# Behind the experts: row statistics on ScalarE, the first values block between the transposes, outputs stored by tile

## The reference

```
x <- LN(a*x + mixer(x));  x <- LN(a*x + memory_cross_attention(x));  x <- LN(a*x + grouped_moe(x))

def post_norm(x, h, g, b):
    z = (DN_ALPHA * x + h).astype(F32)
    mu = jnp.mean(z, axis=-1, keepdims=True)
    var = jnp.mean(jnp.square(z - mu), axis=-1, keepdims=True)
    z = (z - mu) * lax.rsqrt(var + LN_EPS)
    return (z * g.astype(F32) + b.astype(F32)).astype(x.dtype)

def gla_mixer(x, s0, w_in, w_gk2, b_gk2, norm_g, w_out):   # token mixer of layer two
    proj = x @ w_in
    q, k, v, gate, lr = jnp.split(proj, [hk, 2 * hk, 2 * hk + hv, 2 * hk + hv + D_MODEL], axis=-1)
    gk = jax.nn.log_sigmoid((lr @ w_gk2 + b_gk2).astype(F32)) / B_GATE_NORMALIZER
    ...
```

## Time and profile before

| | |
|---|---|
| median of 3 runs | 1459.6 us (1458.09 to 1459.87) |
| profiled execution, its own time | 1458.91 us |
| span of that execution, first to last instruction | 1457.2 us |
| mean granted TensorE clock | 0.987 of 2.4 GHz |
| busy: TensorE, VectorE, ScalarE, POOL | 1374.1, 1034.4, 749.1, 121.2 us |
| HBM traffic over the span | 235 GB/s |

### The profile page before, as it was taken

How to read it: one execution, slowest core, us unless ns; L and a number is a source line. 1 busy time by engine, 2 the same in 40 slices (tenths; PEclk the granted TensorE clock), 3 DMA queues, 4 the chain that set the end, 5 groups by cost and what they waited for, 6 DMA issues and landing times.

```text
span 1457.2 us, 19818 instructions
## 1 busy us (share of the span) xinstructions
PE 1374.1 (94%) x7772; PEld 1145.4 (79%) x7772; DVE 1034.4 (71%) x1121; ACT 749.1 (51%) x764; POOL 121.2 (8%) x195
## 2 busy tenths in 40 slices
PE   6999999999889999999998999999889999999993
PEld 5879898779767788888886988679767788888882
DVE  4444776683548889898987555781658989898985
ACT  4344643333433777676773532331424776676761
POOL 6000045400000000000000023100000000000000
PEclk9999999999999999999999999999999999999997
DMA  8774454434873699888882354445872799898961
GB/s 245 258 238 148 146 189 123 142 108 181 341 310 116 257 335 335 327 338 321 340 319 97 103 185 165 150 151 201 322 286 87 297 326 343 328 331 332 334 246 37
DMA packets 99682, 343.71 MB, mean 236 GB/s; under 512 B 5968, under 2 KB 32096, under 8 KB 70416
## 3 DMA queue, kind: packets, MB, share of 16 engines
q1 hardware_dynamic: 96048, 330.59, 63.1%
q0 software_dynamic: 3552, 11.99, 2.6%
HBM read 327.61 MB, written 14.94 MB: 235 GB/s over the span
## 4 chain that ended last, share of the span: by engine, by line
PE 81%; DVE 11%; ACT 4%; issue 1%; DMA 1%; POOL 0%; SPq 0%; DVEq 0%; ACTq 0%
PE ps L1668 63%; PE ps L1981 2%; PE ps L2126 2%; DVE x L1149 1%; DVE x L1146 1%; DVE stats L1125 1%; PE ps L2168 1%; PE ps L1751 1%; PE ps L2003 1%; PE ps L2038 1%; DVE mix_s L1391 1%; PE ps L1677 1%; PE ps L1991 1%; PE ps L2068 1%; PE ps L1676 1%
## 5 line engine op out<-in xcount | busy, mean ns | idle before, releaser
L1668 PE MATMUL ps<-w_hi,xt_hi 128*128 128x512 f32 x704 | 280.6, 399 | 13.5 <-DVE w_lo L1088 7.7
L1668 PE MATMUL ps<-w_hi,xt_lo 128*128 128x512 f32 x704 | 276.7, 393 | 0.0
L1088 DVE TENSOR_TENSOR w_lo<-raw,w_hi 128x2048 fp32r<-128x2048 f32 x68 | 155.4, 2294 | 158.6 <-ACT w_hi L732 158.6
L1668 PE MATMUL ps<-w_lo,xt_hi 128*128 128x512 f32 x640 | 251.6, 393 | 0.0
L732 ACT ACTIVATE w_hi<-raw 128x2048 fp32r<-128x2048 f32 x68 | 129.3, 1913 | 175.2 <-PE ps L1668 88.0
L1092 DVE TENSOR_TENSOR moe_lo<-moe_in_raw,w_hi 128x2048 fp32r<-128x2048 f32 x72 | 164.3, 2290 | 30.2 <-ACT w_hi L739 30.1
L1092 DVE TENSOR_TENSOR w_lo<-raw,w_hi 128x2048 fp32r<-128x2048 f32 x72 | 164.9, 2292 | 27.4 <-ACT w_hi L739 26.9
L1668 PEld LDWEIGHTS ps<-w_hi,xt_hi 128*128 128x128 f32 x704 | 133.3, 189 | 44.6 <-issue 8.5
L739 ACT ACTIVATE w_hi<-moe_in_raw 128x2048 fp32r<-128x2048 f32 x72 | 138.4, 1922 | 50.4 <-PE ps L1668 50.4
L1668 PEld LDWEIGHTS ps<-w_hi,xt_lo 128*128 128x128 f32 x704 | 133.0, 189 | 29.7
L739 ACT ACTIVATE w_hi<-raw 128x2048 fp32r<-128x2048 f32 x72 | 137.4, 1911 | 12.6 <-PE ps L1668 12.6
(11 more groups left out here) (369 smaller groups left out, 2370.8 us busy)
## 6 DMA issues: line engine op xcount, KB each, us to landing
raw<-in_moe_w_gate SPq DMA_DIRECT2D x48, 1024.0 KB, 4.9
moe_in_raw<-in_moe_w_down SPq DMA_DIRECT2D x48, 1024.0 KB, 4.9
moe_in_raw<-in_moe_w_up SPq DMA_DIRECT2D x32, 1024.0 KB, 4.9
raw<-in_moe_w_up SPq DMA_DIRECT2D x32, 1024.0 KB, 4.9
raw<-in_xattn_w_kv SPq DMA_DIRECT2D x16, 1024.0 KB, 5.9
raw<-in_hgrn_w_in SPq DMA_DIRECT2D x16, 1024.0 KB, 5.6
raw<-in_cache_mem_k SPq DMA_DIRECT2D x16, 1024.0 KB, 5.0
moe_in_raw<-in_moe_w_gate SPq DMA_DIRECT2D x16, 1024.0 KB, 4.9
```

What stands on the lines that cost most here:

```text
L1088: nc.vector.tensor_tensor(lo_at(slot_of(k)), raw_at(slot_of(k)), hi_at(hi_slot(k)).bitcast(F32), ALU.subtract).then_inc(w_low, 1)
L1668: ins = mm(out, lhs, rhs, start=start and n == 0, stop=stop and n == 2, skip_group_check=shared)
```

## The change

Four things, all behind the experts.

1. The third norm's row statistics go from VectorE to ScalarE (`tile_sums`): a Copy with scale -1/1024 that also sums (the negated mean), a Square with that as bias that also sums, Ln, Exp. VectorE keeps scale and shift (`tile_scale`). ScalarE starts a tile when that tile's two sums are added.
2. The splits of layer two's first three chunks move into the last visit of layer one's experts (`split_next`).
3. Layer two's blocks run v, v, k, q, gate, gate. The first values block runs by row tile between the transposes (`turn_next`, `first_values`); the transposes go to other banks (`turn_bank0`). Behind it come the low-rank product and the second values block, with the four decay products in its middle, two PSUM banks in place of four; decay work of ScalarE and VectorE goes behind the two values blocks, key and query products from the first values block to the first gate block.
4. The outputs are stored by row tile from SP, each when its tile is done.

The diff, without the lines that only follow from these:

```diff
 def block_kind(l, n):
-    kinds = [("f", 2), ("v", 2), ("q", 2), ("gate", 2)] if l == 0 else [("k", 1), ("q", 1), ("v", 2), ("gate", 2)]
+    kinds = [("f", 2), ("v", 2), ("q", 2), ("gate", 2)] if l == 0 else [("v", 2), ("k", 1), ("q", 1), ("gate", 2)]
...
 def turns(u, t):
+def turn_bank0(u, t):
+    return (4, 6, 3)[t] if u == 4 else (0, 2, 7)[t]
 def at(static, groups, per):
...
+            for t in range(TILES):
+                sp.wait_ge(ln_done, TILES * (3 * LAYERS - 1) + t + 1)
+                rows = a["y_prompt"][0, t * P:(t + 1) * P, :] if t < 2 else a["y_sample"].rearrange("b t c -> (b t) c")
+                sp.dma_start(rows, x[0:live(t), t, :]).then_inc(y_out, 16)
+            sp.wait_ge(y_out, 16 * TILES)
...
-                if l == LAYERS - 1:
-                    pool.wait_ge(ln_done, TILES * 6)
-                    pool.dma_start(a["y_prompt"][0].rearrange("(t p) c -> p t c", p=P), x[:, 0:2, :]).then_inc(y_out, 16)
-                    pool.dma_start(a["y_sample"].rearrange("b t c -> (b t) c"), x[0:64, 2, :]).then_inc(y_out, 16)
-                    pool.wait_ge(y_out, 32)
...
+            def split_next(n, g):
+                k = CHUNKS0 + n
+                act.wait_ge(loaded[slot_of(k)], at(16 * loads_of(k) + 16 * GCH // MR, g, 16 * GCH // MR))
+                act.wait_ge(w_used, at(CHUNKS0 + GCH - MH + n + 1, g, GCH))
+                nc.scalar.activation(hi_at(hi_slot(k)), raw_at(slot_of(k)), ACT.Copy).then_inc(w_high, 1)
             def split_ahead(db, groups, more=5):
...
+            def tile_sums(l, t, added):
+                n, q = live(t), 3 * l + 2
+                act.wait_ge(mo[l]["read"], added)
+                rows, aside = x[0:n, t, :], st_moe["h"][0:n].rearrange("p e f -> p (e f)")
+                nc.scalar.activation(aside, rows, ACT.Copy, scale=-1.0 / D, accum_out=mean_var[0:n, t, 0:1]).then_inc(ln_mean, 1)
+                act.wait_ge(ln_mean, TILES * l + t + 1)
+                nc.scalar.activation(aside, rows, ACT.Square, bias=mean_var[0:n, t, 0:1], accum_out=mean_var[0:n, t, 1:2]).then_inc(ln_var, 1)
+                act.wait_ge(ln_var, TILES * q + t + 1)
+                rs = rstd[0:n, t:t + 1]
+                nc.scalar.activation(rs, mean_var[0:n, t, 1:2], ACT.Ln, bias=ln_eps[0:n, 0:1], scale=1.0 / D).then_inc(act_step, 1)
+                act.wait_ge(act_step, TILES * q + t + 1)
+                nc.scalar.activation(rs, rs, ACT.Exp, scale=-0.5).then_inc(ln_rstd, 1)
...
-                if l == 1:
+                def decay_args():
                     act.wait_ge(mx_lr, 1)
                     nc.scalar.activation(m["lr_t"], ps[0:16, 7, 0:NT], ACT.Copy).then_inc(mx_lrc, 1)
                     for hh in range(4):
                         act.wait_ge(mx_z, hh + 1)
-                        nc.scalar.activation(m["b"][:, hh, :], ps[:, 4 + hh, 0:NT], ACT.Abs, bias=b_gk[:, hh:hh + 1]).then_inc(mx_lrc, 1)
+                        nc.scalar.activation(m["b"][:, hh, :], ps[:, (3, 7)[hh % 2], 0:NT], ACT.Abs, bias=b_gk[:, hh:hh + 1]).then_inc(mx_lrc, 1)
+                def decay_logs():
                     act.wait_ge(mx_lrc, 5)
                     nc.scalar.activation(m["b"][:], m["b"][:], ACT.Exp, scale=-1.0).then_inc(mx_lrc, 1)
...
+                        if l == 1:
+                            (decay_args, decay_logs)[c]()
...
+                        elif l == 0 and j + MH - GCH < NH:
+                            split_next(j + MH - GCH, g)
...
-                    for k in range(NH):
-                        split(CHUNKS0 + k, groups)
-                layer_norm(3 * l + 2, 4 if l == 0 else None)
+                tile_sums(l, 0, nl * 12 + 14)
+                tile_sums(l, 1, nl * 12 + 16)
+                if l == 0:
+                    turned(4, 0)
+                tile_sums(l, 2, nl * 12 + 18)
+                if l == 0:
+                    turned(4, 1)
+                    turned(4, 2)
...
             def split_expert(k, j, g):
+            def split_next(n, g):
+                k = CHUNKS0 + n
+                dve.wait_ge(w_high, at(k + GCH + 1, g, GCH))
+                nc.vector.tensor_tensor(lo_at(slot_of(k)), raw_at(slot_of(k)), hi_at(hi_slot(k)).bitcast(F32), ALU.subtract).then_inc(w_low, 1)
             def split_ahead(db, groups, more=5):
...
+            def tile_scale(l, t):
+                n, q = live(t), 3 * l + 2
+                dve.wait_ge(ln_in, 32 * (q + 1))
+                dve.wait_ge(ln_mean, TILES * l + t + 1)
+                if t:
+                    dve.wait_ge(ln_done, TILES * q + t)
+                aside = st_moe["xg"][0:n, :]
+                link(nc.vector.scalar_tensor_tensor(out=aside, in0=x[0:n, t, :], scalar=mean_var[0:n, t, 0:1], in1=ln_gb[0:n, 0, :],
+                                                    op0=ALU.add, op1=ALU.mult))
+                dve.wait_ge(ln_rstd, TILES * q + t + 1)
+                nc.vector.scalar_tensor_tensor(out=x[0:n, t, :], in0=aside, scalar=rstd[0:n, t:t + 1], in1=ln_gb[0:n, 1, :],
+                                               op0=ALU.mult, op1=ALU.add).then_inc(ln_done, 1)
...
-                if l == 1:
+                def decay_mins():
                     for hh in range(4):
                         dve.wait_ge(mx_lrc, hh + 2)
-                        ins = nc.vector.tensor_scalar(m["e"][:, 1, hh, :], ps[:, 4 + hh, 0:NT], b_gk[:, hh:hh + 1], 0.0, ALU.add, ALU.min)
+                        ins = nc.vector.tensor_scalar(m["e"][:, 1, hh, :], ps[:, (3, 7)[hh % 2], 0:NT], b_gk[:, hh:hh + 1], 0.0, ALU.add, ALU.min)
                         ins.then_inc(mx_min, 1)
+                def decay_scans():
                     dve.wait_ge(mx_min, 4)
                     dve.wait_ge(mx_ln, 3)
                     link(nc.vector.scalar_tensor_tensor(out=m["b"][:], in0=m["b"][:], scalar=-1.0, in1=m["e"][:, 1], op0=ALU.mult, op1=ALU.add))
...
-                    elif l == 1 and kind == "v" and c == 0:
-                        dve.wait_ge(evac[0], first_block(1) // 2 + 1)
-                        dve.wait_ge(evac[1], first_block(1) // 2 + 1)
+                    elif l == 1 and kind == "gate" and c == 0:
+                        dve.wait_ge(evac[0], first_block(1) // 2 + 2)
+                        dve.wait_ge(evac[1], first_block(1) // 2 + 2)
...
+                        if l == 1:
+                            (decay_mins, decay_scans)[c]()
...
+                        elif l == 0 and j + MH - GCH < NH:
+                            split_next(j + MH - GCH, g)
...
-                    dve.wait_ge(s["read"], nl * 12 + 18)
-                    for c in range(2):
-                        ins = tile_stats(t, c)
-                    link(ins)
-                    tile_norm(3 * l + 2, t)
+                    tile_scale(l, t)
...
-                    for k in range(NH):
-                        split(CHUNKS0 + k, groups)
...
+                    def decay(hh):
+                        if hh < 2:
+                            pe.wait_ge(mx_lrc, 1)
+                        else:
+                            pe.wait_ge(mx_lrc, hh)
+                            pe.wait_ge(mx_min, hh - 1)
+                        mm(ps[:, (3, 7)[hh % 2], 0:NT], w_gk[:, hh * P:(hh + 1) * P], m["lr_t"], start=True, stop=True).then_inc(mx_z, 1)
-                    pe.wait_ge(mx_lrc, 1)
-                    for hh in range(4):
-                        mm(ps[:, 4 + hh, 0:NT], w_gk[:, hh * P:(hh + 1) * P], m["lr_t"], start=True, stop=True).then_inc(mx_z, 1)
-                for nb in range(IN_BLOCKS[l]):
+                    db = first_block(1) + 1
+                    pe.wait_ge(evac[1], db // 2)
+                    for kt in range(KT):
+                        k = chunk_no(db) + kt // 4
+                        if kt % 4 == 0:
+                            pe.wait_ge(w_low, at(k + 1, groups, GCH))
+                        for t in range(TILES):
+                            ins = tile_products(1, slot_of(k), hi_slot(k), kt % 4, kt, t)
+                        if kt % 4 == 3:
+                            ins.then_inc(w_used, 1)
+                        if kt in (3, 5):
+                            decay(kt - 3)
+                            decay(kt - 2)
+                for nb in range(2 * l, IN_BLOCKS[l]):
-                    if l == 1 and nb == 1:
-                        pe.wait_ge(mx_min, 4)
-                        pe.wait_ge(xt_pad, l + 1)
+                        pe.wait_ge(xt_pad, 1)
+                    if l == 1 and nb < 4:
+                        pe.wait_ge(mx_min, nb + 1)
...
-                    for t in range(TILES):
-                        keep_busy((20, 8, 13)[t], 4)
-                        turn(2, 4, t)
+                    db = first_block(1)
+                    def turn_next(t):
+                        pe.wait_ge(ln_done, TILES * 2 + t + 1)
+                        n = live(t)
+                        per = NB // n
+                        for kt in range(KT):
```

(29 more changed lines are left out.)

2 lines of the change are left out of this document (added).

## The result

The changed kernel takes 1434.11 us (median of four executions, 1431.92 to 1435.86); the kernel before took 1459.45 in the same comparison (four, 1458.09 to 1459.87). The profiled execution took 1435.86 with a span of 1434.1, 23.1 less than the span before.

A forecast was written before the change was run, and what follows sets the result against it. TensorE held 81% of the chain, VectorE 11%, with gains where VectorE held it: 10.0 us at the layer boundary plus 7.5 at the end, 17.5 in all, giving 1442.1 us; range 1438 to 1450.

The forecast's parts named there:

- +0.3 at the low half of the sums: Layer one's last expert visit: VectorE's third early weight split delays the low half of the output sums by 0.3 us.
- ScalarE 3.05 per tile: Third norm: ScalarE's row statistics take about 3.05 us per tile with semaphores, bounds 2.55 and 3.2.
- rival 2: ScalarE becomes the norm's bound; at 3.6 per tile the end loses 1.6 us: 1444; counted inside the forecast's 0.64.
- First values from 790.1: Layer boundary: TensorE starts layer two's values at about 790.1, once tile 0's low half is ready, and need not wait thereafter.
- The decay wait: First decay matmul, layer two: ScalarE's low-rank copy ends about 816.0, TensorE arrives 817.6; cover 1.5 us.
- rival 1: Layer two's input blocks: the wait before the decay matmuls and clock drops take part of the gain: 1445 to 1450; chance 0.22.
- POOL's levels until 880.0: Behind the key and query products: POOL's two level builds end at 880.0, TensorE needs them at 883.85; cover 3.8 us.
- rival 3: Middle gains nothing, mixer heads waiting for POOL's levels; only the end's gain remains: 1452, up to 1457; chance 0.08.
- Gain 10.0 us: Layer boundary to the end of the six input blocks: 883.85 against 893.88, 1.7 of it the low clock at 806 to 810.
- The remaining 3.1 to the span's end I keep: Kernel's end: the 3.1 us between the last store's landing and the span's end stay unchanged.
- Everything behind shifts as a whole: After the input blocks: mixer heads, attention and experts are released by TensorE's progress and shift together, with no further gain.
- gain larger than summed: Whole kernel: the gain exceeds the summed 17.5 us if clock drops elsewhere go too; chance 0.03.

The follow-up runs named there:

- pool_by_tile: Changed kernel with its output stores still by tile, but issued by POOL in place of SP: 1437.35 us.
- pool_waits: Changed kernel where POOL too waits for the landing of SP's three stores before its program ends: 1438.40 us, one execution.
- before_pad: Kernel before plus an unused tensor of one element per partition where the change put ln_eps: 1454.13 us beside 1455.53.
- pool_whole: Changed kernel with output stores put back: from POOL after the third tile, one of 1 MB and one of 256 KB: 1440.12 us.
- before_sp: Kernel before with only the changed kernel's stores, by tile from SP: 1451.71 us beside 1458.31, ratio 0.9966.

## Why the prediction was wrong

**Right, step by step.** +0.3 at the low half of the sums: 0.29. ScalarE 3.05 per tile: 2.89 from tile to tile. VectorE idles 0.20 in front of the last shift; the profile names its own scale, but the shift starts 0.68 behind the start of ScalarE's last Exp here (1428.84 to 1429.52) and 0.68 to 0.69 in the eight other profiles with the statistics on ScalarE, so it waits for rstd: rival 2 is real but small. First values from 790.1: 789.71, the values block done at 806.15 for 806.6. The decay wait: ScalarE's low-rank copy ended at 815.4, TensorE came at 817.20, no stall, so rival 1 stayed out. POOL's levels until 880.0: 879.5, ahead of 883.84, so rival 3 stayed out. The store's landing, taken at 2.8: 2.9.

**"Gain 10.0 us" at the boundary.** The mechanism held. It measured 9.47 from the copy of the sums; the end at 883.84 for 883.85 is partly luck, as the copy itself came 0.57 earlier. And it holds only against executions of the old code with the low clock at 806 to 810: four of the eight profiles with the old boundary show it (116.65 to 116.69), four do not (115.14 to 115.17), so the drop is worth 1.5, where 1.7 were counted. Against those without it the boundary gains 8.0. (The block of 14.65 is 14.58 by the prediction's own terms, a difference that changes nothing.)

**"The remaining 3.1 to the span's end I keep."** This failed: 0.4 in place of 3.1, 2.7 of the miss. The prediction read the tail as that of any kernel's end, and its "POOL held nothing behind its stores" passed over the `wait_ge` for their landing that POOL held there. pool_by_tile and pool_waits show that the tail is there when POOL's program ends behind the landing, whoever issued the store, and pool_waits beside the changed kernel that it is gone when SP alone waits.

**"Everything behind shifts as a whole."** This failed, as the prediction's last sentence feared: the experts of layer two became 1.75 shorter, and those of layer one, which lie ahead of the boundary, 1.58, together 3.33 of the miss (3.50 from the first Silu of layer one). The prediction costed instructions and put the new tensor, ln_eps, at nothing without a word. Its allocation moved every tensor behind it by 32 bytes, and before_pad shows that the same padding alone makes the experts 1.58 and 1.75 quicker.

**The rest.** 17.5 + 2.66 + 3.33 - 0.53 - 0.17 make 22.8; the other 0.3 to the 23.1 of the spans is the balance of the two stages of other work (-1.01 and 1.32). What is between 23.1 and the 25.3 of the medians is the choice of execution: the profiled one of the changed kernel is the slowest of its four, at a mean granted clock of 0.992 where the quickest has 0.997. In the next set the medians differ by 21.1 (1455.53 and 1434.39). The forecast's "gain larger than summed", given 0.03, was the case, for other reasons than the one named.

**Open:** by what mechanism the tensors' places set the pace of the matmuls. The passes of VectorE and ScalarE keep their lengths, but no run here parts contention with the loads or with those passes from an effect within TensorE's own reads.

## What to carry to other kernels

Ask of the last wait of each engine's program what the profile shows behind it: a tail between the last landing and the end of the span can belong to the engine that waits, and goes when another engine waits. Part the span at marks that the change does not touch before believing in a sum: here 3.3 us came from stages whose instructions are the same, and an unused tensor in the old kernel showed it in one run. When a small tensor is added, measure what its place does in this way.

## What the runs showed of the hardware that was not expected

- When POOL ends its program behind a wait for a landing, the span ends 2.9 to 3.2 us after the landing (before, pool_whole, pool_by_tile, pool_waits); with SP as the only one waiting for it 0.4 (changed kernel, before_sp).
- The same fp32 matmuls of 128x512 took 8.27 to 8.36 us for a group of 36, and layer one's expert stage 271.7 to 274.2 us, by moves of 32 or 64 bytes of their tensors; the granted clock read 1.00 in all of them. The Trainium skill, SBUF — State Buffer, section SBUF: two separate sides, says that TensorE's ports wait on nobody and that transfers and engines cannot slow each other. By that no other engine and no transfer would be the cause; the runs show a difference of up to 0.9%, and do not show where it comes from.
- Apart from the first 120 us and the last 15, windows of 10 us that hold a drop of the clock read mostly 0.83 to 0.86, and the drops come at a handful of places (near 370, 420, 800, 940, 1020 and 1070 us), in one execution and not in the next; the one at 800 costs 1.5 us. That one is in four of the eight profiles with the old boundary and in none of the eight that keep the change's boundary whole.
